# Layer 1's gate modulation moved from layer 0's router to the change of layers, in a two-layer diffusion trunk

## The chip, the cores and the metric

One core of a Trainium2 chip runs the whole program, one launch for both layers. The metric is the device time in microseconds. The core has TensorE (matrix products, PE in the profile), VectorE (DVE), ScalarE (ACT), GpSimd (POOL) and SyncE (SP, which here only starts transfers). The engines run their own instruction streams and meet through semaphores.

## The reference, cut to what matters

128 context tokens and 128 latent tokens of 1024 features (two groups) pass two layers. Everything is float32.

```python
def layer(x, cond, l, p, ctx):
    mod = jnp.einsum('...d,de->...e', jax.nn.silu(cond), p['w_ada'][l]) + p['b_ada'][l]
    sh1, sc1, g1, sh2, sc2, g2 = jnp.split(mod.reshape(-1, 1, 6 * D_MODEL), 6, axis=-1)
    hn = rmsnorm(x, p['norm_mix'][l]) * (1.0 + sc1) + sh1
    mix, ctx_tensors = token_mixers(hn, l, p, ctx)
    x = x + g1 * mix
    hn = rmsnorm(x, p['norm_ffn'][l]) * (1.0 + sc2) + sh2
    return x + g2 * moe(hn, l, p), ctx_tensors
```

`token_mixers` is one projection by `w_in` (3840 columns), three mixers side by side (differential attention, retention, HGRN2) and one projection by `w_out`. `moe` routes each token to two of 16 experts and adds act(h w_gate, h w_up) w_down of each, weighted. The modulation needs only `cond`, so it can be computed at any time before it is read: `w_ada` of a layer is 24 MB, `w_in` 15 MB, `w_out` 4 MB, the experts 96 MB.

## The kernel before, in words

**Weights.** All weights come through buffers of 1 MB (128 partitions x 2048 numbers). Eight of them are the ring (slots 0 to 7); slots 8 to 12 are eP's second half, wT, home_qc, home_ra and home_kd, which serve other uses in the mixing. SP starts one transfer per buffer, in a fixed order, and waits before each until TensorE has released the slot (`slot{s}_used`); this wait holds up everything behind it on SP. Eight more buffers (`KEPT`: e0, kc, es, wT, e1, hn, xy, fa) take one load each, the twelfth of each expert turn.

**Modulation.** `w_ada` of a layer is handled in three lots: "x" (first shift and scale), "g" (both gates) and "y" (second shift and scale). A lot is eight steps; a step is one 1 MB load and four matmuls with a 32-wide stationary tile (silT), which add up in bank 1 of PSUM (in the profile `ps<-ring,silT`, where each matmul has two records). ScalarE then copies bank 1 out: to modX for x and y, which TensorE transposes and VectorE turns into columns (`modulation_by_feature`), to modG for g (`gate_rows`), where POOL adds the bias by transfers, stores the rows to a scratch tensor (`gates_out`) and later loads them spread over all partitions: gate 1 into xy before the first residual, gate 2 into eP's first half (buffer e0) before the second.

**Order of a layer.** First the norm hn1 (VectorE scales the rows, TensorE transposes them, VectorE and ScalarE write the columns hnT). Then the blocks of `w_in` in the order f, q, a, b, i, r, v, s. The levels of HGRN2 (seven, for two groups) are woven into a, b and i; the attention into r, v and s. `ADA_BEHIND` says how many modulation steps stand behind each block. Then `w_out`, the residual, the norm hn2, the router, and the expert turns: eight turns of two experts, 12 loads each. In the router TensorE computes the scores, VectorE a chain of some 40 small operations that gives each token its seats; zero matmuls (`ps<-zero`) fill some of TensorE's waits.

**Where layer 1's modulation stands.** Lot x in the mixing of layer 0. Lot g in layer 0's router (`next_layers`, `IN_ROUTER`): two steps between the transposes of hn2, one between the scores of the two groups, five behind the row transposes. Lot y: four steps at the change of layers (`at_change`), between the last turn and the first transposes of hn1, and four behind blocks a, a, b and i.

**Turns.** TensorE gathers the tokens of turn 0 (`gather`, `ps<-proj,xs`), transposes the seats of turns 0 and 1 (`ps<-c_begin,proj`) for POOL's indirect gathers and for the scatter, and then runs the turns: gate and up products by eight loads, down products by four, in the order of `TURN_ORDER`. SP's loop starts the next turn's load of a slot as soon as the slot is released. Positions 0 to 10 of a turn are slots, position 11 is the kept buffer of that turn. `FIRST_SLOT` is the ring slot at which a layer begins; it follows from the number of loads of the layers, so that the slots that come free first meet the first loads of the turns.

## Time and profile before

| | us |
|---|---|
| runs of the kernel before | 940.92, 943.03, 1791.33 |
| their median | 943.03 |
| profiled execution | 940.4 |
| its span in the trace | 938.6 |
| TensorE busy in it | 875.3 (93%) |
| VectorE busy | 455.9 (49%) |
| mean granted TensorE clock | 0.99 of full speed |
| moved by transfers | 309.47 MB, 330 GB/s over the span |

Times below are microseconds from the start of the span. A matmul record overlaps the next one, so a busy TensorE can still be one that is late or early for others; what it waited for stands in brackets behind a row of the timeline, "[idle before <-releaser]". "x16" counts records, and the second number of a timeline row is the time from the first start to the last end.

### The profile page before, as it was taken

How to read it: one execution, taken by the hardware profiler on the slowest of the kernel's cores; microseconds unless marked ns; L12 is line 12 of the kernel's file. 1: busy time of each engine (PE TensorE's matmuls, PEld its weight loads, DVE VectorE, ACT ScalarE, POOL GpSimd, SP SyncE). 2: the span in 40 equal slices, each digit the busy share in tenths (PEclk: the TensorE clock that was granted, in tenths of full speed). 3: DMA queues.
4: the chain of work that ended last, by engine and by line, in shares of the span. 5: the costliest groups of instructions: out<-in, count | busy, mean ns of one | idle time of the engine just before them, and what ended most of it. 6: DMA issues, size and time to landing. Idle time of an engine off the chain costs nothing.

```text
span 938.6 us, 13217 instructions
## 1 busy us (share of the span) xinstructions
PE 875.3 (93%) x4735; PEld 445.3 (47%) x4735; DVE 455.9 (49%) x839; ACT 158.2 (17%) x408; POOL 83.8 (9%) x118
## 2 busy tenths in 40 slices
PE   5899999999889999997998999998988999999897
PEld 1655575568543333332335555755864333333232
DVE  2386887652553322332036988877256322333222
ACT  2202024320211110101102120442030111110010
POOL 1112230000010000002000223100001000000001
PEclk9899999999999999999999999999999999999999
DMA  9996674878999999999997353174757999999992
GB/s 361 413 403 272 225 258 192 336 292 341 375 421 421 421 419 421 421 421 410 417 421 304 119 198 133 46 302 175 314 191 279 422 419 421 421 419 422 417 421 104
DMA packets 51020, 309.47 MB, mean 330 GB/s; under 512 B 8866, under 2 KB 8882, under 8 KB 17552
## 3 DMA queue, kind: packets, MB, share of 16 engines
q1 hardware_dynamic: 42368, 291.52, 76.6%
q0 software_dynamic: 5552, 14.52, 4.2%
q10 hardware_dynamic: 3040, 2.62, 0.8%
q8 instruction: 39, 0.64, 0.3%
q14 instruction: 21, 0.17, 0.1%
HBM read 307.56 MB, written 4.75 MB: 333 GB/s over the span
## 4 chain that ended last, share of the span: by engine, by line
PE 60%; DMA 20%; DVE 13%; ACT 3%; issue 2%; SPq 1%; DVEq 0%; ACTq 0%
PE ps L482 57%; DMA ring<-in_w_experts 15%; DMA wT<-in_w_in 3%; PE ps L517 3%; DMA ring<-in_w_ada 2%; ACT eP L1677 2%; DVE proj L1590 1%; DVE rt L1125 1%; DVE eP L1435 1%; DVE fa L1254 1%; DVE hnT L1179 1%; DVE fa L1337 1%; DVE eP L1433 1%; DVE stat L1125 1%; ACT sq L1713 0%
## 5 line engine op out<-in xcount | busy, mean ns | idle before, releaser
L482 PE MATMUL ps<-ring,proj 128*64 128x512 f32 x1024 | 317.0, 603 | 16.5 <-issue 7.6
L482 PE MATMUL ps<-ring,hnT 128*128 128x512 f32 (+1 forms) x576 | 202.3, 503 | 2.0 <-ACT hnT L1798 0.9
L482 PEld LDWEIGHTS ps<-ring,proj 128*64 128x64 f32 x1024 | 97.9, 138 | 156.6 <-issue 156.5
L482 PEld LDWEIGHTS ps<-ring,hnT 128*128 128x128 f32 x576 | 106.3, 190 | 75.2 <-issue 67.1
L1648 DVE COPY proj<-ps 128x512 f32<-128x512 f32 x16 | 11.1, 692 | 127.0 <-PE ps L482 127.0
L482 PE MATMUL ps<-home_kd,proj 128*64 128x512 f32 x128 | 57.7, 593 | 3.4 <-DMA ring<-in_w_experts 3.4
L482 PE MATMUL ps<-ring,silT 128*32 128x512 f32 x384 | 47.7, 617 | 12.8 <-DVE silT L1142 6.7
L482 PE MATMUL ps<-home_ra,proj 128*64 128x512 f32 x128 | 57.7, 594 | 0.0
L482 PE MATMUL ps<-home_qc,proj 128*64 128x512 f32 x128 | 57.6, 593 | 0.0
L1634 DVE RECIPROCAL proj<-proj 128x512 f32<-128x512 f32 x16 | 53.7, 3353 | 0.6
L1633 DVE TENSOR_SCALAR proj<-proj 128x512 f32<-128x512 f32 x16 | 6.8, 427 | 87.8 <-ACT proj L1677 87.8
L482 PE MATMUL ps<-hnT,ring 128*128 128x256 f32 x192 | 43.6, 382 | 0.0
L482 PE MATMUL ps<-proj,modX 128*128 128x512 f32 x80 | 38.7, 606 | 0.0
L482 PEld LDWEIGHTS ps<-hnT,ring 128*128 128x128 f32 x192 | 35.7, 190 | 5.9 <-issue 1.2
L482 PEld LDWEIGHTS ps<-home_kd,proj 128*64 128x64 f32 x128 | 17.3, 137 | 40.9 <-issue 34.3
L1638 DVE TENSOR_TENSOR proj<-ps,proj 128x512 f32<-128x512 f32 x16 | 11.1, 692 | 52.5 <-PE ps L482 52.5
L1923 ACT COPY proj<-ps 128x512 f32<-128x512 f32 x16 | 9.4, 585 | 161.1 <-PE ps L517 161.1
L482 PEld LDWEIGHTS ps<-xy 64*128 64x128 f32 (+1 forms) x480 | 29.9, 188 | 12.0 <-issue 11.1
L1916 ACT COPY proj<-ps 128x512 f32<-128x512 f32 x32 | 18.7, 585 | 93.9 <-PE ps L517 75.5
L482 PEld LDWEIGHTS ps<-home_qc,proj 128*64 128x64 f32 x128 | 17.4, 137 | 35.7 <-issue 35.7
L482 PE MATMUL ps<-xy 64*128 64x64 f32 (+1 forms) x480 | 32.0, 275 | 0.1
L1677 ACT ACTIVATE proj<-ps 128x512 f32<-128x512 f32 x16 | 9.6, 597 | 129.3 <-PE ps L482 129.3
(260 smaller groups left out, 1059.2 us busy)
## 6 DMA issues: line engine op xcount, KB each, us to landing
ring<-in_w_experts SPq DMA_DIRECT2D x128, 1024.0 KB, 18.8
ring<-in_w_ada SPq DMA_DIRECT2D x48, 1024.0 KB, 11.5
ring<-in_w_in SPq DMA_DIRECT2D x24, 1024.0 KB, 7.2
home_qc<-in_w_experts SPq DMA_DIRECT2D x16, 1024.0 KB, 16.2
home_ra<-in_w_experts SPq DMA_DIRECT2D x16, 1024.0 KB, 19.2
home_kd<-in_w_experts SPq DMA_DIRECT2D x16, 1024.0 KB, 18.9
ring<-in_w_out SPq DMA_DIRECT2D x8, 1024.0 KB, 11.5
eP<-in_w_experts SPq DMA_DIRECT2D x4, 1024.0 KB, 10.4
```

What stands on the lines that cost most here:

```text
L482: ins = nc.tensor.matmul(*a, **k)
L517: last = nc.tensor.transpose(ps[:, b, i * P:(i + 1) * P], src, C["ident"][:])
L1125: return v.tensor_reduce(out=out, in_=in_, axis=AX, op=op)
L1179: ins = ts(hnT[:, kc, tok(g)], ps[:, b, k * P:(k + 1) * P], modT[:, 2 * a + 1, kc, one(g)], modT[:, 2 * a, kc, one(g)], ALU.mult, ALU.add)
L1254: st(v.reciprocal(R, R))
L1337: v.copy_predicated(out=half_blocks(A[:, g], lv, 1 - r), mask=mask, data=ps[:, bank, 0:256].rearrange("p (h n b) -> p h n b", h=HR, b=b)). ...
L1634: st(v.reciprocal(ge, ge))
L1638: tt(act, ps[:, 3], gs, ALU.mult).then_inc(c.freed(("gu", 1), "act"), 1)
L1648: v.tensor_copy(ys[:, 1], ps[:, 3]).then_inc(c.freed(("yP", 1), "ys", 1), 1)
L1677: return act_(out, in_, AF.Exp, scale=scale, **k)
L1916: evac(("xT", half), None, "xTs", half, fn=lambda src: nc.scalar.copy(xT[:, KH * half:KH * (half + 1), :], src.rearrange("p (k s) -> p k s ...
L1923: evac(("actT",), None, "actTs", fn=lambda src: nc.scalar.copy(actT, src.rearrange("p (k s) -> p k s", k=KE)))
```

## The change

Lot g of layer 1 moves out of layer 0's router to the change of layers, all eight steps of it. Lot y of layer 1 is no longer at the change: its eight steps stand behind blocks b (3), i (3) and r (2). With the eight loads out of layer 0's router the ring slots of both layers shift, and both orders of the turns are now of one form: home_qc, four early ring slots, home_ra, home_kd, then the other four. In both layers the seats of turns 0 and 1 are transposed behind the first pair of weights of turn 0, into bank 1, instead of ahead of it into bank 3. POOL loads gate 2 after the seventh turn's kept buffer (xy) is released, instead of the first one's (e0). Layer 0's router gets two zero matmuls more at two places, and five in place of two modulation steps. ScalarE copies layer 1's gates out behind block a of layer 1, and POOL counts what it has seen with a few more increments.

```diff
-TURN_ORDER = ((10, 11, 12, 0, 1, 2, 3, 4, 5, 6, 7),
-              (10, 2, 3, 4, 5, 11, 12, 6, 7, 0, 1))
+TURN_ORDER = ((10, 2, 3, 4, 5, 11, 12, 6, 7, 0, 1),
+              (10, 4, 5, 6, 7, 11, 12, 0, 1, 2, 3))
...
-ADA_BEHIND = ((2, 3, 3, 3, 3, 2, 4, 4), (0, 0, 2, 1, 1, 0, 0, 0))
-GATES_AHEAD = 0
-AT_CHANGE = 4
-FIRST_SLOT = (6, 0)
+ADA_BEHIND = ((2, 3, 3, 3, 3, 2, 4, 4), (0, 0, 0, 3, 3, 2, 0, 0))
+AT_CHANGE = 8
+FIRST_SLOT = (0, 2)
...
-        IN_CHANGE = [(1, "y", k) for k in range(AT_CHANGE)]
-        IN_ROUTER = [(1, "g", k) for k in range(GATES_AHEAD, KC)]
+        IN_CHANGE = [(1, "g", k) for k in range(AT_CHANGE)]
+        LATER = [[(0, "g", k) for k in range(KC)] + [(0, "y", k) for k in range(KC)] + [(1, "x", k) for k in range(KC)],
+                 [(1, "g", k) for k in range(AT_CHANGE, KC)] + [(1, "y", k) for k in range(KC)]]
...
-                if l + 1 < L:
-                    normalized_group("hn2", "xn2", 1, lambda b: next_layers(2))
-                else:
-                    normalized_group("hn2", "xn2", 1, lambda b: stream_zeros(b, 5))
+                normalized_group("hn2", "xn2", 1, lambda b: stream_zeros(b, 5))
...
-                    if g:
-                        next_layers(1)
...
-                    next_layers(KC)
                     modulation_by_feature(l + 1, 0, 3)
                 pe.wait_ge(S("bank2_free"), c.claim(2))
-                stream_zeros(2, 9 if l else 5)
+                stream_zeros(2, 9 if l else 7)
...
-                stream_zeros(0, 5 if l else 3)
+                stream_zeros(0, 5)
...
                     gather()
-                    led.turn = 1
-                    pe.wait_ge(c.of("seatG", 0), c.at("seatG", 0))
-                    bank_of_transposes(("seatT",), [a[:, g, :] for a in (seatG, picked_token) for g in range(NG)], 3)
...
                             for half in range(2):
+                                if not t and not i and half:
+                                    led.turn = 1
+                                    pe.wait_ge(c.of("seatG", 0), c.at("seatG", 0))
+                                    bank_of_transposes(("seatT",), [a[:, g, :] for a in (seatG, picked_token) for g in range(NG)], 1)
+                                    led.turn = t
...
-                if l == 0:
-                    gate_rows(0)
+                gate_rows(l)
...
-                if l + 1 < L:
-                    gate_rows(l + 1)
...
-                pool.wait_ge(S("e0_spent"), c.cum[l + 1])
+                pool.wait_ge(S("xy_spent"), c.cum[l + 1])
```

How the rows move is shown at three places. A row names the line, the operation, what it writes and reads, and the tile's shape; x8 counts equal instructions. The first is TensorE in layer 0's router, from the wait for the second group's norm to the first product of the seats; before:

```order
L482 MATMUL ps<-ring,silT 32x512 x8
L549 MATMUL ps<-c_begin,xs 128x128 x8
L482 MATMUL ps<-zero 128x512 x4
L482 MATMUL ps<-c_later,hnT 128x16 x8
L482 MATMUL ps<-ring,silT 32x512 x4
L482 MATMUL ps<-c_later,hnT 128x16 x8
L517 MATMUL ps<-c_begin,hnT 128x128 x16
L482 MATMUL ps<-ring,silT 32x512 x20
L594 MATMUL ps<-c_begin,modX 128x128 x4
L482 MATMUL ps<-zero 128x512 x5
L482 MATMUL ps<-rt,c_later 128x32
```

The same place in the changed kernel, TensorE:

```order
L470 MATMUL ps<-zero 128x512 x5
L537 MATMUL ps<-c_begin,xs 128x128 x8
L470 MATMUL ps<-zero 128x512 x4
L470 MATMUL ps<-c_later,hnT 128x16 x16
L505 MATMUL ps<-c_begin,hnT 128x128 x16
L582 MATMUL ps<-c_begin,modX 128x128 x4
L470 MATMUL ps<-zero 128x512 x7
L470 MATMUL ps<-rt,c_later 128x32
```

The 32 matmuls of the eight gate steps are gone from between the transposes, the scores and the rows; the order of the rest is the same. The second place is SP's queue at the change of layers, behind its loop; before:

```order
L385 DMA eP<-in_w_in 128x2048
L385 DMA wT<-in_w_in 128x2048
L384 ISA
L385 DMA ring<-in_w_ada 128x2048 x4
L385 DMA ring<-in_w_in 128x1024 x2
L384 REGISTER_ALU
L385 DMA ring<-in_w_in 128x2048 x2
L385 DMA ring<-in_w_ada 128x2048 x2
```

And in the changed kernel, SP:

```order
L383 DMA eP<-in_w_in 128x2048
L383 DMA wT<-in_w_in 128x2048
L382 ISA
L383 DMA ring<-in_w_ada 128x2x1024 x6
L382 REGISTER_ALU
L383 DMA ring<-in_w_ada 128x2x1024 x2
L383 DMA ring<-in_w_in 128x1024 x2
L383 DMA ring<-in_w_in 128x2048 x4
L382 REGISTER_ALU
L383 DMA ring<-in_w_ada 128x2048 x3
```

Eight loads of w_ada stand between block f and block q instead of four, and blocks q, a and b then follow in one piece. The third place is TensorE in layer 1's mixing, from the second half of block a for the latent tokens, behind HGRN2's diagonal products, through block b and its steps (`ps<-xy 128x64` are the levels); before:

```order
L482 MATMUL ps<-ring,hnT 128x512 x4
L482 MATMUL ps<-ring,silT 32x512 x8
L482 MATMUL ps<-ring,hnT 128x512 x4
L482 MATMUL ps<-xy 128x64 x16
L482 MATMUL ps<-ring,hnT 128x512 x4
L482 MATMUL ps<-xy 128x64 x16
L634 REGISTER_ALU
L482 MATMUL ps<-ring,hnT 128x512 x4
L482 MATMUL ps<-xy 128x64 x16
L482 MATMUL ps<-ring,hnT 128x512 x4
L482 MATMUL ps<-xy 128x64 x16
L482 MATMUL ps<-ring,silT 32x512 x4
```

And in the changed kernel, TensorE, up to the steps behind block b:

```order
L470 MATMUL ps<-ring,hnT 128x512 x8
L470 MATMUL ps<-xy 128x64 x16
L470 MATMUL ps<-ring,hnT 128x512 x4
L470 MATMUL ps<-xy 128x64 x16
L615 REGISTER_ALU
L470 MATMUL ps<-ring,hnT 128x512 x4
L470 MATMUL ps<-xy 128x64 x16
L470 MATMUL ps<-ring,hnT 128x512 x4
L470 MATMUL ps<-xy 128x64 x16
L555 REGISTER_ALU
L484 REGISTER_ALU
L470 MATMUL ps<-ring,silT 32x512 x12
```

The two steps behind block a are gone, and behind block b three stand where one stood.

## Rows read from the trace of the kernel before

**Rows 1.** The page: GB/s in 40 equal slices of 23.5 us.

```profile
GB/s 361 413 403 272 225 258 192 336 292 341 375 421 421 421 419 421 421 421 410 417 421 304 119 198 133 46 302 175 314 191 279 422 419 421 421 419 422 417 421 104
```

**Rows 2.** Timeline, TensorE, last scatter of layer 0: start, duration, group.

```profile
488.16 3.80 PE L482 MATMUL ps<-proj 128*128 128x512 f32 x8
```

**Rows 3.** Chain of waits, change of layers: start, duration, what.

```profile
477.13 18.65 DMA ring<-in_w_ada
...
496.89 0.60 PE ps L549 x4
```

**Rows 4.** Timeline, SP's transfers, start and end of both loops.

```profile
270.60 0.35 SPq L468 DMA_DIRECT2D home_qc<-in_w_experts  x1
...
440.31 21.84 SPq L468 DMA_DIRECT2D ring<-in_w_experts  x8
...
717.48 0.35 SPq L468 DMA_DIRECT2D home_qc<-in_w_experts  x1
...
901.74 0.33 SPq L468 DMA_DIRECT2D ring<-in_w_experts  x1
```

**Rows 5.** Transfers issued 270.5 to 271: count, size, us to landing.

```profile
home_qc<-in_w_experts SPq DMA_DIRECT2D x1, 1024.0 KB, 10.1
```

**Rows 6.** Transfers issued 717 to 718.

```profile
home_qc<-in_w_experts SPq DMA_DIRECT2D x1, 1024.0 KB, 5.9
```

**Rows 7.** Last loop load of layer 0 (462 to 463); layer 1's (901.7) reads alike.

```profile
ring<-in_w_experts SPq DMA_DIRECT2D x1, 1024.0 KB, 19.0
```

**Rows 8.** Transfers issued 421 to 424, POOL's and SP's.

```profile
eP<-gates POOLq DMA_DIRECT2D x2, 512.0 KB, 12.9
ring<-in_w_experts SPq DMA_DIRECT2D x1, 1024.0 KB, 24.9
```

**Rows 9.** Timeline, TensorE, layer 0, seat transposes ahead of turn 0.

```profile
263.53 0.65 PE L517 MATMUL ps<-c_begin,proj 128*128 128x128 f32 x4 [1.40 <-DVE proj L1590]
```

**Rows 10.** The same in layer 1.

```profile
712.99 0.65 PE L517 MATMUL ps<-c_begin,proj 128*128 128x128 f32 x4 [0.94 <-DVE proj L1590]
```

**Rows 11.** Timeline, VectorE: hn2 columns (both layers), first SwiGLU of layer 0.

```profile
238.94 2.77 DVE L1179 TENSOR_SCALAR hnT<-ps,modT 128x128 f32<-128x128 f32 x8
...
271.90 0.43 DVE L1633 TENSOR_SCALAR proj<-proj 128x512 f32<-128x512 f32 x1 [4.29 <-ACT proj L1677]
...
691.50 2.77 DVE L1179 TENSOR_SCALAR hnT<-ps,modT 128x128 f32<-128x128 f32 x8
```

**Rows 12.** Timeline, TensorE, layer 1's mixing: modulation steps, attention values.

```profile
538.93 1.92 PE L482 MATMUL ps<-ring,silT 128*32 128x512 f32 x16
...
563.04 1.06 PE L482 MATMUL ps<-ring,silT 128*32 128x512 f32 x8
...
584.35 1.07 PE L482 MATMUL ps<-ring,silT 128*32 128x512 f32 x8
...
627.07 2.00 PE L482 MATMUL ps<-proj,wT 128*128 128x64 f32 x16 [1.55 <-DVE proj L1298]
```

**Rows 13.** Timeline, VectorE, layer 1's mixing.

```profile
545.77 1.09 DVE L1331 TENSOR_TENSOR xy<-xy,fa 128x256 f32<-128x256 f32 x1 [1.26 <-PE ps L482]
...
569.39 0.50 DVE L1331 TENSOR_TENSOR xy<-xy,home_es 128x256 f32<-128x256 f32 x1 [1.00 <-PE ps L482]
...
586.20 0.69 DVE L1407 COPY home_qc<-ps 128x512 f32<-128x512 f32 x1
...
614.76 0.69 DVE L1298 COPY proj<-ps 128x512 f32<-128x512 f32 x1 [0.21 <-PE ps L482]
...
618.92 0.20 DVE L1427 RECIPROCAL rt<-rt 128x8 f32<-128x8 f32 x1 [1.20 <-ACT eP L1677]
```

**Rows 14.** TensorE's clock: two timeline rows; a window (PE, PEld, DVE, ACT, POOL, PEclk, DMA, GB/s).

```profile
6.65 1.93 PE L482 MATMUL ps<-ring,silT 128*32 128x512 f32 x8 [6.65 <-DVE silT L1142]
...
438.49 5.35 PE L482 MATMUL ps<-ring,proj 128*64 128x512 f32 x16 [3.54 <-DMA ring<-in_w_experts]
...
358.00:360.00 2.00, 2.00 (x6) 0.60 (x4) 0.00 (x0) 0.00 (x0) 0.00 (x0) 0.50 1.01 422
```

31 lines of the change are left out of this document (8 added, 23 removed).

## The prediction

> **What bounds the kernel now.** I read the page first: the line of memory traffic stands at about 420 GB/s from the eleventh slice to the end of layer 0's turns and again through layer 1's, so both expert stages run at the pace of the transfers, with a gap of two slices (191 and 279) ahead of layer 1's turns [rows 1]. TensorE's own work of layer 0's turns ends at 491.96 [rows 2]. Then the chain of waits at the change of layers: its last 18.65 us are the queue of weight loads, up to the fourth modulation load, and TensorE's first transposes of layer 1 stand at 496.89, 1.1 us behind that landing at 495.8 [rows 3]. Then SP's timeline with the landing times: they tell when the stream of the loop begins and ends [rows 4 to 7]. Then TensorE and VectorE around the two routers [rows 9 to 11] and in layer 1's mixing [rows 12, 13]. The mixing of layer 1 is neither memory nor TensorE alone: VectorE is late in some places, TensorE in others. So the change touches four places, and each has its own limit.
>
> **Router of layer 0 and first turn.** Eight modulation steps (some 0.95 us of TensorE each [rows 12]) leave it. Layer 1's router has no such steps, so it is the model. From the end of VectorE's hn2 columns (694.26) to the transposes of the seats (712.99) it takes 18.73 us there, 21.82 us in layer 0 (241.71 to 263.53) [rows 9 to 11]: 3.1 us go. Four zero matmuls more than layer 0 has now cost nothing against this model, which has them and two more. The seat transposes, behind the gather by 0.94 us of waiting in layer 1, move behind the first pair of weights. Gather's end in layer 0 is then 241.71 + (712.05 - 694.26) = 259.5. The first freed slot's load is issued 717.48 - 712.99 = 4.5 us behind the start of those transposes in layer 1 [rows 4, 10]; 0.65 us of that, their own time, is out as well, so it comes 3.84 us behind the gather, at 263.3 instead of 270.60. The queue is empty there as in layer 1 (the gap of [rows 1]), so the load lands after 5.9 us, not 10.1 [rows 5, 6]: at 269.2 instead of 280.7. The stream is 11.5 us ahead. VectorE handles the seats some 2 us later; its idle time of 4.29 us before the first SwiGLU hides that [rows 11].
>
> **The end of layer 0.** What is left of the stream is the same: 76 loads, the token gathers, gate 2 and the parameters. It ran from 280.7 to 480.8 (last loop load issued at 461.8, 19.0 us to land [rows 4, 7]), so it would end at 480.8 - 11.5 = 469.3. Check with layer 1: 723.4 to 920.7 is 197.3 us, without the parameters. Now the loads that must land before layer 1's first block: two of w_in and four modulation steps took 495.8 - 480.8 = 15.0 us, 2.5 us each. The change makes them ten: 25.0 us, to 494.3, and transposes at 495.4. **Term A is -1.5 us**: eight loads fewer in the router and four more here are four fewer in all (-10 us), but 8.5 us of this is given back as an idle queue between the filled slots and the first turn. With layer 1's slightly better pace it is -2. The slots are free in time: the last one is released by TensorE about 9 us after the last landing, and its load has to start 22 us after it.
>
> Gate 2 is issued about a turn later, then the parameters behind it on POOL. Both still come before the end of the loop's stream, so they still precede the gate loads if the queues share. They did: gate 2 landed in 12.9 us while a weight load issued in that stretch took 24.9 [rows 8]. The Trainium skill (DMA: Bandwidth & Descriptors, "Queues, rings and completion order") says that each engine takes turns between the queues that have work; the rows agree. If POOL's traffic instead waited its turn behind SP's, 2 MB or 4.8 us would drop behind the gates, and A would be -6.3; I keep that as part of the low end. In layer 1 nobody waits for gate 2: issued about with the last loop load at 901.7, it lands near 914.6, before the last weights at 920.7, which its product follows. The parameters are read only after block q. The extra increments on POOL I cost at nothing. Behind the gates SP's queue holds w_in's next blocks: q would land near 497 and a near 502, and block a is in work until 538.93 [rows 12], so they are not late.
>
> **TensorE's clock at the change.** Now TensorE finishes the turns (491.96 now [rows 2], about 480 then) long before the eight loads: it does three steps at once and then one of 0.95 us per 2.5 us until 494.3. The trace has two such stretches: after 3.54 us without work, sixteen matmuls took 5.35 us instead of 3.65, and a window some turns earlier has the granted clock at 0.50, the level of 1.2 GHz [rows 14]. The first step of the program at that level took 1.93 us against 1.06 [rows 12, 14]. So if it falls: +0.9 for the last step, +0.4 for the transposes, +0.7 to +1.7 for the first f matmuls until it is back. **Term B is +2 us**, between 0 (granted clock stays) and +4 (it stays down through both groups of f). I take +2, for the busy share is below 40% over 11 us. The Trainium skill (TensorE: Matmul & The Clock Gate, "Part 1: The HAM clock gate") calls the slow level the default, which activity releases; by that alone B would be above zero too.
>
> **Mixing of layer 1.** Now two second-modulation steps stand behind block a, one behind b, one behind i [rows 12]; then three behind b, three behind i, two behind r: four more, 3.8 us of TensorE. Step by step: without those behind a, TensorE is 1.9 us early and VectorE's wait of 1.26 us shrinks, but the three behind b bring it back to 0 at the fourth level, where VectorE waits 1.00 us [rows 13]. Behind i TensorE is 1.9 us late. VectorE's copy of the first query transposes at 586.20 follows them with some 0.3 us to spare: +1.6. Behind r TensorE is 3.8 late, less 0.75 that it waits for a bank anyway; VectorE meets this at 614.76, but its next wait, 1.20 us on ScalarE, takes the excess up, and at 627.07 TensorE waits 1.55 us for VectorE [rows 12, 13]. **Term C is +1.9 us**, between 0 and all 3.8. The gates' copy to modG now falls on ScalarE behind block a, with nothing behind it that is wanted before block b is done; its reader on POOL comes after the levels. The bank is free when the first step of b wants it.
>
> **First turn of layer 1.** The wait of 0.94 and the transposes' 0.65 leave the way of the first slot; the turns are a memory stream to 920.7, so all of it moves: **term D is -1.6 us**, 0 if the stream starts no earlier. Layer 1's router is otherwise as it was. Gate 2 only changes places within the stream.
>
> **Sum.** -1.5 + 2 + 1.9 - 1.6 = +0.8 us on the profiled execution's 940.4 (a span of 938.6 and 1.8 around it): 941.2. The two usual runs, 940.92 and 943.03, lie 0.5 and 2.6 above the profiled one; I add 0.8 for a median: **942.0**. Two per cent, about what a measurement of this kernel can tell from no change, is 19 us, more than all terms together.
>
> **Rivals.** (1) The clock holds, or the steps hide in VectorE's waits: B or C is 0, the time 938 to 940. For it: TensorE's waits at the change are 1.5 us each, shorter than the one before the low clock. 22%. (2) The queue never runs empty in layer 0, or POOL's loads fall behind the gates: A is -6 to -10 and the time 933 to 937.5. Against it stands layer 1's gap [rows 1]; for it, only that layer 0's loads start earlier against its router. 9%. (3) Slower: the trickle of gate loads leaves TensorE at 1.2 GHz through both f groups (B = +4) and the added steps all show (C = 3.8). Place: the chain from 495 to 509, which is short matmuls between waits, with little to bring the clock back. It decides as soon as B + C passes 3.1. -1.5 + 4 + 3.8 - 1.6 = +4.7: 945 to 947. 17%. (4) Something outside these four places (a slot that is not freed in time and stops SP's queue) or over 2% either way: 4%.
>
> The forecast, 940 to 944, has the remaining 48%. The range 936 to 947 leaves out most of (2) and of (4) and a piece of (3).
>
> **What the next profile would show.** The loop's first load issued near 263 and landed near 269; the last near 469; the transposes of layer 1 near 495 to 497, behind a modulation load; a granted clock under 1 between 484 and 500; the distance from there to layer 1's hn2 columns some 2 us longer; the first matmul of layer 1's turns directly behind the gather. The prediction is wrong if the stream of layer 0 is not the limit from 269 on, if its gap is longer than layer 1's, or if the low clock reaches into the mixing.

## The result, and the profile after

The changed kernel takes 945.92 us in the median of 15 runs (943.12 to 948.61), the kernel before 943.03; the ratio is 1.0031, with a 95% interval from 1.0019 to 1.0044. One run of the kernel before took 1791.33 us and is not in the ratio. So the change makes the kernel slower by 0.3%, where I had forecast 942.0. The profiled execution is 944.09 us (span 942.3). A second comparison, with a second profile of each (below), gave 1.0043 (1.0026 to 1.0061).

The page of the changed kernel, GB/s in 40 slices, answers to [rows 1]. The gap ahead of layer 0's turns is deeper (slices 11 and 12 have 289 and 356, where there were 375 and 421), and the plateau of these turns and the modulation loads ends in the same slice 22 as before:

```profile
GB/s 362 414 406 262 223 271 182 332 316 314 289 356 422 419 420 421 420 420 421 412 408 265 137 132 190 214 273 196 285 217 272 422 421 420 420 420 422 420 418 103
```

SP's timeline at both ends of layer 0's loop and at the start of layer 1's [rows 4], and the landing times (count, size, us to landing) of the first loop load of layer 0 and of the last [rows 5, 7]:

```profile
262.66 0.35 SPq L456 DMA_DIRECT2D home_qc<-in_w_experts  x1
...
441.38 4.94 SPq L456 DMA_DIRECT2D ring<-in_w_experts  x3
...
720.54 0.35 SPq L456 DMA_DIRECT2D home_qc<-in_w_experts  x1
```

```profile
home_qc<-in_w_experts SPq DMA_DIRECT2D x1, 1024.0 KB, 4.8
...
ring<-in_w_experts SPq DMA_DIRECT2D x1, 1024.0 KB, 24.0
```

The loop's first load is issued 7.9 us earlier than before and lands at 267.5 instead of 280.7, 13.2 us earlier (0.65 us of this is the earlier hn2 columns, 238.29 against 238.94). The last lands at 446.0 + 24.0 = 470.0, and that is only 10.8 us earlier. The chain of waits at the change of layers [rows 3], and TensorE's timeline there:

```profile
476.85 18.54 DMA ring<-in_w_ada
...
495.43 1.94 PE ps L470 x8
497.37 1.06 PE ps L537 x4
```

```profile
482.64 1.07 PE L470 MATMUL ps<-ring,silT 128*32 128x512 f32 x8 [1.49 <-DMA ring<-in_w_ada]
485.20 1.66 PE L470 MATMUL ps<-ring,silT 128*32 128x512 f32 x8 [1.49 <-DMA ring<-in_w_ada]
487.76 1.94 PE L470 MATMUL ps<-ring,silT 128*32 128x512 f32 x8 [0.90 <-DMA ring<-in_w_ada]
...
495.43 1.94 PE L470 MATMUL ps<-ring,silT 128*32 128x512 f32 x8 [0.62 <-DMA ring<-in_w_ada]
497.30 1.97 PE L537 MATMUL ps<-c_begin,xs 128*128 128x128 f32 x8
```

The eight gate loads land 2.56 us apart, the last at 495.4, where the fourth y load had landed at 495.8. The step at 485.2 takes 1.66 us and those from 487.8 on 1.94 us instead of 1.07: the clock is at its half level, 1.2 GHz. The windows of the same stretch say so directly, and show that TensorE had been busy 3.60 of 6 us before it fell (columns: PE, PEld, DVE, ACT, POOL, PEclk, DMA share, GB/s); the last row is another place, in block s of layer 1's mixing:

```profile
478.00:484.00 6.00, 3.60 (x26) 0.47 (x24) 4.99 (x7) 3.29 (x8) 2.18 (x2) 1.00 1.02 406
484.00:490.00 6.00, 3.59 (x16) 0.36 (x16) 0.00 (x0) 0.00 (x0) 0.00 (x0) 0.63 1.03 413
490.00:496.00 6.00, 4.44 (x20) 0.61 (x24) 0.00 (x0) 0.00 (x0) 0.00 (x0) 0.50 1.03 415
496.00:500.00 4.00, 3.39 (x18) 1.70 (x12) 1.42 (x5) 0.00 (x0) 0.00 (x0) 0.60 1.02 421
645.00:650.00 5.00, 4.66 (x11) 2.44 (x12) 4.17 (x9) 1.59 (x3) 0.00 (x0) 0.66 0.28 105
```

Then layer 1's mixing: TensorE's y steps [rows 12], then VectorE's rows that answer to 586.20 and 618.92 in [rows 13], and the next hn2 columns [rows 11]:

```profile
585.70 2.78 PE L470 MATMUL ps<-ring,silT 128*32 128x512 f32 x24
...
606.32 1.92 PE L470 MATMUL ps<-ring,silT 128*32 128x512 f32 x16
...
589.17 0.69 DVE L1384 COPY home_qc<-ps 128x512 f32<-128x512 f32 x1 [1.66 <-PE ps L505]
...
622.29 0.20 DVE L1404 RECIPROCAL rt<-rt 128x8 f32<-128x8 f32 x1 [0.57 <-ACT eP L1654]
...
696.12 2.77 DVE L1156 TENSOR_SCALAR hnT<-ps,modT 128x128 f32<-128x128 f32 x8
```

Where VectorE had read the query transposes without a wait, it now waits 1.66 us for them. Its distance to the old times grows from 1.34 us at its copy before (581.90 against 580.56) to 2.97 us there, is 3.37 at the reciprocal and 4.62 at the columns.

To compare whole executions I cut each span at the same seven events: VectorE's second hn2 columns of layer 0; the first loop load of layer 0; TensorE's step on the last modulation load at the change; VectorE's first read of block f in layer 1; the second hn2 columns of layer 1; the first loop load of layer 1; the end. The second profile of each kernel, from the experiments, stands beside the first. The pieces, in us, each worked out from two rows:

| piece | before | before, again | after | after, again | mean change |
|---|---|---|---|---|---|
| start to hn2 of layer 0 (same in both) | 238.94 | 240.89 | 238.29 | 239.32 | -1.1 |
| router 0 | 31.66 | 31.83 | 24.37 | 25.14 | -7.0 |
| turns 0 and modulation loads | 225.23 | 224.55 | 232.77 | 233.11 | +8.1 |
| to block f | 13.36 | 13.37 | 14.69 | 13.93 | +0.9 |
| mixing, w_out, hn2 of layer 1 | 182.31 | 182.33 | 186.00 | 184.44 | +2.9 |
| router 1 | 25.98 | 26.02 | 24.42 | 24.31 | -1.6 |
| turns 1 and end | 221.12 | 221.01 | 221.76 | 221.55 | +0.6 |

The first row is chance: two profiles of the kernel before differ there by 1.95 us, and over all profiles below both arrangements need 239.6 us in the mean to this point (ten with the new one, three with the old one that move no work ahead of it). The others add up to +3.9 us. My four terms stand in them one by one: A in rows two and three (+1.1 instead of -1.5), B in the fourth (+0.9, +2 forecast), C in the fifth (+2.9, +1.9 forecast), D in the last two (-1.0, -1.6 forecast).

### The profile page after: what moved, and what is told of

The parts are those of the page before. It is cut to its first block, busy times and chain, and to the rows that moved or that the text cites. A ratio compares the mean times of both kernels' runs of the same rounds, so it can differ in the third digit from the quotient of the medians.

```text
span 942.3 us, 13164 instructions
## 1 busy us (share of the span) xinstructions
PE 877.4 (93%) x4744; PEld 444.5 (47%) x4744; DVE 457.6 (49%) x839; ACT 158.4 (17%) x408; POOL 83.8 (9%) x118
## 4 chain that ended last, share of the span: by engine, by line
PE 69%; DMA 17%; DVE 7%; SPq 3%; ACT 2%; issue 2%; DVEq 0%; ACTq 0%
PE ps L470 66%; DMA ring<-in_w_experts 8%; DMA home_ra<-in_w_experts 5%; DMA wT<-in_w_in 3%; PE ps L505 3%; SPq L383 3%; DMA ring<-in_w_ada 2%; ACT eP L1654 1%; DVE hnT L1156 1%; DVE rt L1102 1%; ACT sq L1690 0%; DVE stat L1102 0%; DVE xs L1129 0%; DVE eP L1412 0%; PE ps L537 0%
## 5 line engine op out<-in xcount | busy, mean ns | idle before, releaser
L470 PE MATMUL ps<-ring,proj 128*64 128x512 f32 x1024 | 339.4, 595 | 4.0 <-DMA home_ra<-in_w_experts 2.3
L470 PEld LDWEIGHTS ps<-ring,proj 128*64 128x64 f32 x1024 | 103.1, 137 | 140.1 <-issue 139.3
L470 PE MATMUL ps<-ring,silT 128*32 128x512 f32 x384 | 51.9, 657 | 17.8 <-DMA ring<-in_w_ada 11.2
L470 PE MATMUL ps<-home_kd,proj 128*64 128x512 f32 x128 | 57.8, 594 | 11.5 <-issue 6.1
L470 PEld LDWEIGHTS ps<-ring,silT 128*32 128x32 f32 x384 | 10.1, 113 | 49.4 <-DMA ring<-in_w_ada 24.3
## 6 DMA issues: line engine op xcount, KB each, us to landing
ring<-in_w_ada SPq DMA_DIRECT2D x48, 1024.0 KB, 11.2
```

The lines of the kernel that those rows point to most:

```text
L470: ins = nc.tensor.matmul(*a, **k)
```

## The experiments

All compare with the kernel before on the same chip. Each set had another chip or time, so medians of different sets differ by a microsecond or more, and the ratios are the better guide. The first set has no run of the changed kernel itself: its variants can be held against 1.0031 and 1.0043 only, which were taken elsewhere.

**First set: one part undone or covered.** Back to the old place of the seat transposes:

```
                     gather()
+                    led.turn = 1
+                    pe.wait_ge(c.of("seatG", 0), c.at("seatG", 0))
+                    bank_of_transposes(("seatT",), [a[:, g, :] for a in (seatG, picked_token) for g in range(NG)], 3)
...
-                                if not t and not i and half:
...
-                                    bank_of_transposes(("seatT",), [a[:, g, :] for a in (seatG, picked_token) for g in range(NG)], 1)
```

> The changed kernel with one part undone: the transposes of the seats stand ahead of turn 0 again, in bank 3, in both layers. All else is as changed (median 945.9 us, 2.9 us above the kernel before). Theory 1, the prediction's term D: the wait (0.94 us) and the transposes (0.65 us) come back onto the way of the first freed slot, and the turns of layer 1 are a memory stream, so all 1.6 us show: 947.5, and the distance from layer 1's gather to the issue of the first slot's load grows from 7.7 to about 9.3 us. Theory 2: only the wait comes back, because the 0.65 us of the transposes stand in the way of the third and fourth slot in the changed kernel anyway (its stream ran 3.66 us late in mid-turns where its first load was only 3.06 us late): about 946.9. Theory 3: the start of the stream doesn't set its end, 945.9. The same edit in layer 0 adds 0.6 to 1.6 us there by theories 1 and 2, since its end is a memory stream too; so up to 949 in all by theory 1 and 947.8 by theory 2.

Measured: 951.15 us (944.49 to 956.2), ratio 1.0097 (1.006 to 1.0134). Slower, as all but theory 3 said, and by more than any: its runs scatter over 12 us. Its profile (span 949.2) has 27.53 us in router 0, against 24.4 to 25.5 in the first set's other three kernels and the changed one, and 25.48 in router 1 against some 24.4 (but 26.48 in the kernel with short y steps), so 2 and 1.1 us go there; 232.01 for the turns of layer 0 gives 0.9 of it back. The rest, some 3 us in the median, isn't explained by the parts it restores. The profile has the clock at half in more places, behind the last wait too (0.81 to 0.85 granted from 920 to 930), and its six runs go with their mean clock: 944.49 and 947.25 us at 0.988, 956.2 at 0.974. Term D has the right sign at the first load, with 1.1 of the 1.6 us.

Zero matmuls at the change:

```
                     for step in IN_CHANGE:
                         ada_step(*step)
+                        stream_zeros(b, 5)
```

> The changed kernel with five matmuls on zeros (some 1.1 us) behind each of the eight gate steps at the change of layers, into the bank that the transposes take next; the result is the same. Theory 1, the prediction's term B with the size that the trace gave: TensorE's granted clock stays at 1.00 from 484 to 500, the last gate step takes 0.95 instead of 1.94 us, the transposes 1.1 instead of 1.97, and the end comes 1.3 us earlier, 944.6. Rival: the clock is not what makes the changed kernel late there; the zeros only fill the wait, and behind the last step they even add up to 1.1 us: 945.9 to 947.

Measured: 946.86, ratio 1.0064 (1.0044 to 1.0084). No gain. The profile shows the clock at 1.00 and all steps at 1.07 us, but from the last step to block f it takes 14.39 us, against 13.36 to 14.71 in kernels without the zeros: the five behind the last step cost the 1.0 us that the clock gave back.

One quarter of four y steps, the other three quarters of these products left out:

```
-                for j in range(4):
+                for j in range(1 if (l, what) == (1, "y") and 2 < k < 7 else 4):
```

> The changed kernel with four of layer 1's eight steps of the second shift and scale (k = 3 to 6) cut to one of their four matmuls, so that about 2.85 us of TensorE's work go while every load stays; three of the four quarters of these products are left out. It takes back most of the four steps that the change adds to layer 1's mixing. Theory 1: that stretch is bound by TensorE and the steps show in full (the trace has layer 1's VectorE 2.4 us further behind from 534 to 615 by them): -2.4 to -2.9, 943.3. Rival, the prediction's term C as it was sized: half of them lies in waits: -1.4, 944.5. Rival 2: a clock that falls near 645 costs 1.5 us whatever stands before it; then the profile shows it here too, at the same place of the program.

Measured: 946.97, ratio 1.0059 (1.0039 to 1.0080). The first two expectations rested on 2.85 us leaving TensorE, and none left; the third, a low clock near 645 whatever stands before it, isn't borne out by this profile, whose mixing takes 184.42 us. TensorE's timeline of this kernel, three steps behind block i, of one matmul each (two records a matmul):

```profile
586.89 2.76 PE L470 MATMUL ps<-ring,silT 128*32 128x512 f32 x6
```

Twelve matmuls take 2.78 us (585.70 above), three take 2.76. The four quarters of a step run side by side on 32 columns of the array each, and one alone is as long. The Trainium skill (TensorEngine Tiling (Array Packing), "Tiling Modes") lists a split into four tiles of 32 columns; this is its number here. The run says nothing on term C.

The transposes one pair further back:

```
-                                if not t and not i and half:
+                                if not t and i and not half:
```

> The changed kernel with the seat transposes one pair further back, behind the second pair of weights (before the third). Theory 2 of the first run of this set: in the changed kernel the transposes hold up the second pair by 0.65 us while the memory queue holds only two loads; one pair further on, four loads are in it and nothing is held up, so each layer's stream is up to 0.65 us earlier: about 944.6 to 945.3. Rival: the queue had enough at that point and only the start counts, 945.9. Rival 2: the rows of turn 1 are fetched too late now, since their numbers hang on these transposes, and turn 0 waits for them: 946.5 or more.

Measured: 946.20, ratio 1.0058 (1.0038 to 1.0079). No gain by the time. In its profile, router 0 to the last modulation load is 258.4 us, inside the 257.1 to 259.8 of the others, and layer 1's turns are 221.46 against 221.76, which is within what two profiles differ.

**Second set: the two kernels again, and two cleaner tests.** The first two are the changed kernel and the kernel before, unedited.

> The changed kernel once more, for a second profile beside the others of this set on one chip. The comparison gave 1.0031 of the kernel before, and the first set's variants of the changed kernel stood at 1.006 of it with 946.2 to 947.0 us. If that set was ordinary, this one gives 1.003 to 1.006 again. In its profile, theory: the time from layer 1's second columns to its router is longer by 2.46 us of TensorE work whatever the clock does, and the rest of the difference between two profiles lies where the granted clock is at half: in the router of layer 0 (0 or 1.1 us), at the change (0 to 1.35), in block s near 650 (0 or 1.5) and elsewhere. Rival: another stretch differs that no low clock accounts for.

> The kernel before once more, for a second profile and the clock of each of its runs: ratio 1.000. Theory: its eight gate steps keep TensorE at work in layer 0's router, so the granted clock stays at 1.00 between the second hn2 columns and the gather there (18 us), and at the change of layers; the changed kernel's variants had a low stretch in this router in four of five profiles. Its mean clock over its runs is then above the changed kernel's by about 0.005, which is 10 us at half clock, worth some 2 us. Rival: the low stretches fall on both kernels alike, and the mean clocks agree.

Measured: the changed kernel 946.24, ratio 1.0043 (1.0026 to 1.0061); the kernel before 942.20, ratio 1.0001 (0.9985 to 1.0018). The two profiles stand in the table. Windows 248 to 252, the middle of layer 0's router: the kernel before again, the changed kernel (first profile), the changed kernel again, and the kernel before with the seats moved (third set, below):

```profile
248.00:252.00 4.00, 3.69 (x32) 2.34 (x35) 2.72 (x15) 2.54 (x5) 0.38 (x1) 1.00 1.02 420
```

```profile
248.00:252.00 4.00, 3.16 (x20) 2.09 (x21) 3.38 (x19) 0.00 (x0) 1.00 (x2) 1.00 0.83 227
```

```profile
248.00:252.00 4.00, 3.18 (x13) 1.92 (x12) 3.35 (x20) 1.17 (x2) 1.07 (x2) 0.50 0.42 98
```

```profile
248.00:252.00 4.00, 4.00 (x21) 2.50 (x24) 3.38 (x19) 2.34 (x4) 0.54 (x1) 0.50 0.95 395
```

And the stretch of that last kernel in which its clock was still up, but for the end:

```profile
238.00:246.00 8.00, 7.54 (x62) 4.90 (x56) 3.71 (x10) 1.86 (x5) 0.00 (x0) 0.99 1.03 424
```

So the half level appears in this router in one profile of the same program and not in another. With the old router full of work it appears too, which my expectation had excluded: TensorE was busy for 7.54 of the 8 us before (the 4.00 of 4.00 behind it are busy partly because everything takes longer at half clock). It costs 2.6 us there (21.99 instead of 19.36 us from the columns to the gather), and 0.8 to 2.4 in the changed router. The forecast that the gate steps keep the clock up there has fallen. The other half of the expectation held: the mean clock is 0.983 over the 15 runs of the result and over the 8 runs here, and 0.989 over the 106 runs of the kernel before in the four sets. Within either kernel, a run whose mean clock is 0.001 lower is longer by 0.4 us; a line through all these runs puts 2.3 us of the difference with the clock and leaves 1.1 us (0.3 to 2.0) at equal clock. That is an estimate from runs that nobody steered, and the next run limits it.

More zeros, none behind the last step:

```
                     for step in IN_CHANGE:
+                        if step[2]:
+                            stream_zeros(b, 5)
                         ada_step(*step)
...
+                    if h and stage == "hn2" and not l:
+                        stream_zeros(b, 4)
...
-                stream_zeros(2, 9 if l else 7)
+                stream_zeros(2, 9)
...
-                stream_zeros(0, 5)
+                stream_zeros(0, 5 if l else 9)
```

> The changed kernel with more matmuls on zeros where TensorE waits, the result the same: five ahead of each gate step at the change but the first (none behind the last, which cost the first version of this 1.0 us), and in layer 0's router four ahead of the second half's transposes, two more ahead of the picks and four more ahead of the gather. Theory: no low clock in that router and at the change: some 1.0 us in the router in most runs and 0 to 1.35 us at the change, together 1.5 to 2 us below the changed kernel of this set. Rival: low stretches fall elsewhere anyway, or the zeros in the router delay what follows them by as much as they save (up to 0.9 us each place): within 0.7 us of the changed kernel.

Measured: 945.43, ratio 1.0040 (1.0022 to 1.0057) beside 1.0043 of the changed kernel: 0.8 us less by the medians, 0.3 by the ratios, so nearest to the rival. What was meant did happen, and over its 12 runs the mean clock is 0.989, as in the kernel before. Yet the time did not come back. So the mean clock is not the price: where it falls counts, and what the zeros themselves take isn't known. Windows of this kernel at the change of layers, and in the last turn:

```profile
484.00:490.00 6.00, 5.64 (x37) 1.44 (x30) 0.00 (x0) 0.63 (x4) 0.00 (x0) 1.00 1.04 412
490.00:496.00 6.00, 5.13 (x30) 1.23 (x28) 0.00 (x0) 0.00 (x0) 0.00 (x0) 1.00 1.03 414
915.00:920.00 5.00, 5.00 (x16) 1.42 (x12) 0.00 (x0) 0.00 (x0) 0.00 (x0) 0.54 0.81 339
```

The last step to block f takes 13.35 us, exactly as before the change, so B is gone. But in this profile the clock fell in the last turn, and there it cost more. The zeros need not be the cause: it fell behind the last wait in three profiles without them too (seats back, short y, small y). TensorE's timeline at that place:

```profile
914.12 1.12 PE L470 MATMUL ps<-home_kd,proj 128*64 128x512 f32 x1 [3.33 <-DMA ring<-in_w_experts]
```

Four y steps almost empty:

```
+                m = 32 if (l, what) == (1, "y") and 2 < k < 7 else BLK
                 for j in range(4):
-                    last = mm(ps[32 * j:32 * j + 32, b, :], silT[:, k, :], cols[:, j * BLK:(j + 1) * BLK], start=(k == 0), stop=(k == KC - 1))
+                    last = mm(ps[32 * j:32 * j + 32, b, 0:m], silT[:, k, :], cols[:, j * BLK:j * BLK + m], start=(k == 0), stop=(k == KC - 1))
```

> The changed kernel with four of layer 1's steps of the second shift and scale (k = 3 to 6) cut to 32 of 512 columns each; 15 of 16 columns of these products are left out. Cutting them to one of four matmuls took no time off (three such steps still took 2.76 us against 2.78, so the four quarters run side by side), so that run said nothing on term C. Now 3.5 of 3.8 us of TensorE's work really go, and all loads stay. Theory: the three behind block i and the one behind r are what made this stretch 2.46 us longer; without them it is that of the kernel before or a little less, 2.0 to 2.5 us below the changed kernel. Rival (term C as sized): 1.0 to 1.9 us; rival 2: nothing, because the other loads and blocks set the pace.

Measured: 944.52, ratio 1.0023 (1.0010 to 1.0037). By the medians 1.7 us below the changed kernel of this set, though the intervals touch. Its profile settles it. TensorE's three steps, and VectorE's copy behind them, which waits for nothing now:

```profile
587.37 0.40 PE L470 MATMUL ps<-ring,silT 128*32 128x32 f32 x24
```

```profile
589.27 0.69 DVE L1385 COPY home_qc<-ps 128x512 f32<-128x512 f32 x1
```

Taken from the second hn1 columns of layer 1, VectorE is 2.42 to 2.47 us late behind the exponentials in the six profiles with full steps in which that event compares, and 0.54 us late here. So C is 2.46 us of TensorE's time: +0.42 by the steps behind b, +1.6 by those behind i, +0.4 by those behind r. 1.9 of it goes with 3.5 us of work.

**Third set: gate 2, the seats alone, the y steps in another place.**

Gate 2's rows are fetched as early as before the change:

```
-                pool.wait_ge(S("xy_spent"), c.cum[l + 1])
+                pool.wait_ge(S("e0_spent"), c.cum[l + 1])
```

> The changed kernel with one part undone: POOL fetches the rows of gate 2 as soon as it may again (when the weights of turn 0 kept in e0 are used up, that is behind the last token gather), and not when those of turn 6 are; in layer 0 the parameters follow it earlier too. Six profiles of the changed kernel and its variants show TensorE waiting 3.2 to 3.5 us for the last load of layer 1 (1.0 to 1.1 in two profiles of the kernel before), and in four of eight a low clock behind that wait, for 1.5 to 2.5 us. Theory: gate 2's megabyte between the last loads makes this one long wait; undone, the wait is 1.1 us again, no low clock follows it, and the time from the first loop load of layer 1 to the last wait's end falls from 196.3 to 195.7: 0.6 to 1.5 us off the changed kernel, 944.7 to 945.6. Rival: the traffic is the same in sum and the low stretches are chance: within 0.5 us of it, 946.2.

Measured: 944.86, ratio 1.0020 (1.0009 to 1.0032). The last wait is short again and the long one is a turn earlier. This kernel, and the changed one and the kernel before at the last wait:

```profile
887.46 1.09 PE L470 MATMUL ps<-ring,proj 128*64 128x512 f32 x1 [3.27 <-DMA home_ra<-in_w_experts]
...
919.55 0.64 PE L470 MATMUL ps<-home_kd,proj 128*64 128x512 f32 x1 [0.95 <-DMA ring<-in_w_experts]
```

```profile
917.03 0.64 PE L470 MATMUL ps<-home_kd,proj 128*64 128x512 f32 x1 [3.20 <-DMA ring<-in_w_experts]
```

```profile
913.34 0.64 PE L482 MATMUL ps<-home_kd,proj 128*64 128x512 f32 x1 [1.13 <-DMA ring<-in_w_experts]
```

From the first loop load to the last wait's end it takes 196.52 us here, 196.49 in the changed kernel, 195.86 in the kernel before. So gate 2's place doesn't make the 0.6 us between the last two; that part of my theory fell. It moves the one wait of 3.2 us, and with it the place at which the clock may fall: in its profile that is behind the wait at 887 (1.09 us a matmul), where the memory stream has the slack to take it up. Behind the last wait nothing takes it up: it was worth 2.2 to 2.7 us in the two profiles in which it fell early there (224.22 and 223.97 us for the last piece of the table, in the runs with zeros and with small steps). The kernel before has such a wait a turn earlier too (2.82 us at 880.86). Over all profiles, the clock fell behind the last wait in four of nine with the late gate 2 and in none of six with the early one. The gain in time is 1.0 to 2.2 us by the ratios, but the intervals overlap, so it is likely and not shown.

Then the kernel before with the seat transposes moved alone, as in the change but in bank 3:

```
-                    bank_of_transposes(("seatT",), [a[:, g, :] for a in (seatG, picked_token) for g in range(NG)], 3)
...
+                                if not t and not i and half:
...
+                                    bank_of_transposes(("seatT",), [a[:, g, :] for a in (seatG, picked_token) for g in range(NG)], 3)
```

> The kernel before with one part of the change alone: the seat transposes and their wait move behind the first pair of weights, in both layers. They go to bank 3 here (bank 1 in the change), which the second half of gate and up of turn 0 takes some 3 us later. Theory, the prediction's term D, which undoing it in the changed kernel bore out with 2 to 3 us in layer 0 and 1.2 in layer 1: 1.6 us off in layer 1 and 1 to 2 in layer 0, less 0.6 for the transposes that now stand between two pairs: 2 to 3 us, 939.3 to 940.3. Rival: bank 3 is not free in time and TensorE waits for VectorE's copy before the second half; the load queue is short then, and half of the gain goes: 941. Rival 2: in layer 0 the queue is still full of the gate steps' loads when the first slot comes free, so only layer 1 gains: 940.7.

Measured: 941.12, ratio 0.9984 (0.9970 to 0.9999). The only kernel here that is faster than both, by 1.5 us, less than the 2 to 3 expected. In layer 1 the way to the first load is 24.47 us instead of 26.0, but the turns take 196.24 to the last wait's end instead of 195.8. SP's timeline of this kernel:

```profile
717.75 0.35 SPq L468 DMA_DIRECT2D home_qc<-in_w_experts  x1
718.35 7.25 SPq L468 DMA_DIRECT2D ring<-in_w_experts  x4
725.78 0.40 SPq L468 DMA_DIRECT2D home_ra<-in_w_experts  x1
```

The first four further loads take 7.25 us to go out, 6.52 in the kernel before: the transposes' 0.7 us still stand between two pairs and hold up the third and later slots. So D is 1.1 us net. In layer 0 this profile shows no gain: the columns to the last modulation load take 258.49 us, with the low clock in the router, against 256.4 and 256.9. Whether the seats gain there at full clock (the second rival says no) stays open.

Two y steps from behind i to behind r:

```
-ADA_BEHIND = ((2, 3, 3, 3, 3, 2, 4, 4), (0, 0, 0, 3, 3, 2, 0, 0))
+ADA_BEHIND = ((2, 3, 3, 3, 3, 2, 4, 4), (0, 0, 0, 3, 1, 4, 0, 0))
```

> The changed kernel with two of the three second shift and scale steps behind block i moved behind r: three behind b, one behind i, four behind r. The profiles have the three behind i as the dear ones: VectorE's offset against the kernel before jumps from +0.43 to +2.05 us there, and reaches +2.46 behind the two of r. Theory: the jump behind i goes (offset 0.4 to 0.5 at the copy of the queries), and the two more behind r cost what exceeds the waits there (TensorE's 0.75, VectorE's 1.2 on ScalarE): offset at the end of the mixing +1.0 to +1.6, so 0.9 to 1.4 us off the changed kernel. Rival: TensorE has no slack between i and r, what leaves one place comes at the other: offset +2.4 and no gain. Rival 2: ScalarE takes the modulation from the bank later and its exponentials wait: +3 or more.

Measured: 945.25, ratio 1.0025 (1.0011 to 1.0039). The trace is with the first rival. VectorE is 0.5 us late behind block i, but 3.17 at its copy behind r and 2.45 after it, to the hundredth what it was with three and two. The next places to the end of the mixing are as late; between b and r TensorE has no slack for a step, wherever it stands. By the ratio the run can't be told from the changed kernel.

**Fourth set: fewer loads behind the router.** Two, and then four, of layer 1's gate steps go to the end of layer 0's mixing (`GATES_AHEAD = 2` or `4`, on the kernel with the seats alone).

> The kernel before with the seat transposes moved as in the run of that part alone (941.1 us), and two of layer 1's gate steps taken out of layer 0's router and put at the end of layer 0's mixing, behind its other modulation steps. Theory on the changed kernel's missing term A: what counts for the end of layer 0 is how many loads the memory moves between the router and layer 1's first block, 2.5 us each; the change only took four out (ten us) and lost ten (an empty queue, a slower start, low clock). Two loads moved ahead of the w_out weights, where the queue moves 211 GB/s, leave that stream for good: -5 us there, against +1.9 us of TensorE ahead of the w_out products and up to 5 us if those weights now land late: -3 at best, 938. Rival: the w_out weights and the first expert loads behind them fill the memory from 200 us to the router (411 to 424 GB/s), so the stream reaches back to there, TensorE waits for w_out by what was put ahead, and the time is within 1 us of 941.1.

> As the run with two gate steps ahead, with four. Theory: twice the gain in the stream (-10 us) and twice the cost (+3.8 us of TensorE), as long as the loads fit into the free time before the w_out weights: 936 to 938. Rival: only about two or three loads fit there (some 9 us of free memory time from 180 to 200), the rest delays w_out, and this one is no better or worse than the one with two: 940 or more. Whichever it is, it tells whether the end of layer 0 is set by the loads behind the router alone, which the undoing of single parts can't tell.

Measured: 942.56, ratio 1.0009 (0.9990 to 1.0028), and 941.96, ratio 0.9990 (0.9977 to 1.0004). Neither is shown to beat the seats alone. The stretch from router 0's columns to the last modulation load got shorter: 255.3 us with two loads fewer and 252.8 with four, against 256.4 to 258.5. What four loads are worth at 2.5 us each went in part into memory standing idle: from the columns to the first loop load it moved 360 GB/s, against 399 to 414 in the others. But the columns themselves came at 243.08 and 244.85 instead of 239 to 241. TensorE's timeline with four ahead, and the kernel before at this place:

```profile
205.50 5.34 PE L482 MATMUL ps<-ring,silT 128*32 128x512 f32 x32 [2.11 <-ACT modX L1691]
210.77 2.43 PE L482 MATMUL ps<-ring,hnT 128*128 128x256 f32 x10
```

```profile
204.88 3.69 PE L482 MATMUL ps<-ring,hnT 128*128 128x256 f32 x16 [0.93 <-ACT hnT L1798]
```

TensorE waits for ScalarE to empty bank 1, then the four steps run (5.34 us, partly at the low clock), and the w_out products come 5.9 us later. So the loads do set the end of layer 0, at 0.9 to 1.4 us each rather than 2.5, and it is TensorE's time that pays for them elsewhere.

## Why the prediction was off, point by point

**The sum and the forecast.** The sum of the terms was +0.8 us. The forecast of 942.0 is still 1.0 below the 943.03 of the kernel before, because I put the sum on the profiled execution (940.4) and added 0.8 for a median, where this kernel's median is 2.6 above it. From the median the same sum gives 943.8. So the sum had the right sign and the forecast had not; the terms then missed by 2.1 us against the result, and by 3.1 against the pieces.

**Term A is the step that failed.** The issue of the first loop load was forecast at 263.3 and came at 262.66; so far the model of layer 1's router was right. What failed are the sentences that the stream is 11.5 us ahead and that what is left of it is the same. I had added to the 7.3 us of the issue the 4.2 us by which the load would land faster, and shifted the whole stream by that. The third loads of the two loops were issued at 271.67 and 266.75, and the queues moved this between the landing of the first load and that of the third (packets, MB, share of 16 engines), in 4.98 us before and in 7.00 us after:

```profile
home_kd<-in_w_experts SPq DMA_DIRECT2D x1, 1024.0 KB, 14.0
...
q1 hardware_dynamic: 288, 2.10, 101.1%
```

```profile
ring<-in_w_experts SPq DMA_DIRECT2D x1, 1024.0 KB, 7.7
...
q1 hardware_dynamic: 337, 2.50, 85.5%
q0 software_dynamic: 144, 0.36, 13.4%
```

The first load lands 13.2 us ahead of the old one, the third 11.2, the last 10.8. Of the 2.0 us lost at once, some 0.9 are the token rows of turn 0 (q0, 0.36 MB): they had landed at 275.2, ahead of the first loop load, and land at 273.8 now, behind it. The rest is 0.40 MB more on the weights' queue for the same two loads: when the first one landed in a queue that had been empty, less of the loads behind it had been moved than is usual in a full one. So the landing of one load in an empty queue is not the same point of the stream as its landing among others.

The whole stretch shows the balance. Windows from the hn2 columns to the first loop load and from there to the last modulation load, before and after:

```profile
238.94:270.60 31.66, 28.18 (x200) 16.51 (x198) 16.98 (x68) 5.80 (x12) 4.11 (x5) 1.00 1.02 414
270.60:495.83 225.23, 210.58 (x929) 76.70 (x925) 67.72 (x94) 24.09 (x43) 13.70 (x17) 0.98 1.01 419
```

```profile
238.29:262.66 24.37, 19.76 (x135) 13.71 (x134) 14.77 (x59) 5.22 (x11) 2.98 (x4) 1.00 0.76 284
262.66:495.43 232.77, 217.37 (x976) 76.81 (x974) 71.63 (x104) 25.67 (x46) 14.81 (x18) 0.98 1.01 415
```

At the old rates the new traffic (6.9 MB, then 96.7 MB) would take 247.4 us, 9.5 less than before. It took 257.1: 7.7 us were lost in the router, where the memory is busy for 0.76 of the time and not all of it, and 2.1 behind it, 0.6 of them because a gate load lands every 2.56 us and a y load every 2.49. Against this stand my -10 and +8.5. The second profile of the changed kernel adds 0.8 us of low clock in the router. So the stretch gave back what the router had gained (-7.0, +8.1), and the four loads fewer bought nothing even at full clock: 256.4 to 256.9 before, and 257.14 in the best of the changed ones.

**Term B** had the right mechanism. The trickle of gate loads brought the clock to half, as [rows 14] had suggested, and it was 1.33 us and 0.56 us in the two profiles of the changed kernel; in some variants it was 0, since the clock was back in time. +2 was too much: I had reckoned with a slow start of block f, and the clock was back for it. The Trainium skill (TensorE: Matmul & The Clock Gate, "Part 1: The HAM clock gate") has the slow level as the default, which activity releases; the windows of 484 to 500 are in line with it, with 0.50 to 0.63 granted behind 3.60 of 6 us of work.

**Term C** was right in its places and low in its size. The 1.6 us at the copy of the queries was measured as 1.6. But I let the first steps and the last cost nothing, and they cost 0.42 and 0.4: 2.46 in sum, 2.1 after a fixed 0.3 that comes back at hn2. To it comes 1.5 us where the clock falls in block s near 650, seen in four of the nine profiles of the new arrangement whose y steps take their full time (the first of the changed kernel among them) and in neither of the kernel before. It isn't proper to the new arrangement, though: the profile with four gate steps ahead has one like it (185.37 us for the mixing, 0.83 granted from 635 to 640). I had not thought of that place.

**Term D** was 1.6 us at the first load and 1.0 at the end. The transposes' 0.65 us left the way of the first slot and stood in that of the fourth; I had counted them as gone.

**Gate 2.** I wrote that nobody waits for it. That is so, but its megabyte now lies between the last loads, and TensorE's last wait for a load (the fourth from the end) is 3.2 us instead of 1.1. The wait costs nothing by itself; what can follow it, the low clock in the last turn, does.

**Rival 3**, with 17%, is the nearest to what happened: slower, by clock and added steps together, with B + C at 3.8 us in the mean of the two profiles, past the 3.1 that I had named. But it had B at 4 and A still at -1.5, so it is near in its time partly by luck: A, 2.6 us off in the pieces, is the largest miss, and with A as forecast the pieces would add up to +1.3. The chance that all stays within 2% held.

Two things stay open: why undoing the seats' move cost some 5 us in time where its profile accounts for 2 to 3, and by how much the changed kernel's median rests on the clock. The parts at full clock sum to +0.3 (A) + 2.1 (C) - 1.6 + 0.5 (D) = +1.3 us, near the 1.1 that the runs leave at equal clock. The 2.9 us measured (4.0 in the second comparison) leave 1.6 to 2.7 for B and the other low stretches. One or two profiles of a kernel can't divide this among their places, and the run that brought the mean clock back did not bring the time back.

## What to carry to other kernels

Compare memory streams at equal points: from the issue of the first load to the landing of the last, with everything that moves between them, never by the landing time of one load. Loads taken out of a stretch give time only if the memory has something else to move there. When work is moved out of a stretch bound by memory into one bound by an engine, price it at the engine's full time, unless a wait of that very engine, and not of its reader, is there to take it; moving it about within the stretch then changes nothing. And when a change turns several short waits of TensorE into one long one, or leaves it a trickle of work, put that place where something slower runs beside it, not at the end of the kernel.

## What the runs showed of the hardware

Four matmuls on 32 columns each take 0.93 us together, and one of the four alone takes 0.92 (2.76 us for three). Cutting the number of columns streamed works instead: 128x32 in place of 128x512 brought three steps from 2.78 to 0.40 us.

A 1 MB load that reads two pieces of each row instead of one (the gate loads beside the y loads of `w_ada`) lands every 2.56 us instead of every 2.49 in a full queue.

TensorE's granted clock fell to its half level in a router in which TensorE had been busy for 7.54 of the 8 us before, and in the changed kernel's router it fell in one profile and not in the other. Two profiles of that kernel differ by 0.8 us in the router and by 0.8 us at the change, where their clocks differ. With zeros at the change it stayed up there and fell in the last turn of that profile.
